# Seven half-block products in place of eight in the feed-forward stages of the second block

## The reference

```python
def _sqrelu_mlp(x, w1, w2):
    return jnp.square(jax.nn.relu(x @ w1)) @ w2
...
for l in range(DEPTH_2):          # two layers
    ...
    x = _layer_norm(ALPHA * x + h, ln_g[l, 0], ln_b[l, 0], LN_EPS)
    x = _layer_norm(ALPHA * x + _sqrelu_mlp(x, mlp_w1[l], mlp_w2[l]), ln_g[l, 1], ln_b[l, 1], LN_EPS)
```

## Time and profile before

| | |
|---|---|
| median of 3 runs | 3240.03 us |
| all runs | 3239.92, 3240.03, 3252.42 us |
| the profiled execution, its own time | 3255.05 us |
| its span, first to last instruction | 3253.3 us |
| PE busy, share of the span | 2929.4 us, 90% |
| DVE busy, share | 815.3 us, 25% |
| ACT busy, share | 530.7 us, 16% |
| DMA, mean over the span | 60 GB/s |
| granted TensorE clock, mean | 0.924 of 2.4 GHz |

### The profile page before, as it was taken

The page is one execution under the profiler, slowest core; times in us unless marked ns, Lnnn a source line. Parts: engine busy times, 40 slices in busy tenths (PEclk is TensorE's granted clock), DMA queues, the critical chain, the costliest instruction groups (busy, mean ns, idle before and its releaser), DMA issues. The chain is left out here.

```text
span 3253.3 us, 39654 instructions
## 1 busy us (share of the span) xinstructions
PE 2929.4 (90%) x17796; PEld 1594.8 (49%) x17796; DVE 815.3 (25%) x1355; ACT 530.7 (16%) x1003; POOL 216.3 (7%) x176
## 2 busy tenths in 40 slices
PE   3999988977899998897888789999989998899997
PEld 2655677753444443344766534444434454344443
DVE  1121233452444401203666420100010162110001
ACT  2111212220100001012444210000010161100001
POOL 0000044520000000001222100000000000000000
PEclk7899868998899999998888789999989999899998
DMA  5122200011122112111000011222212201122110
GB/s 250 52 104 104 78 2 2 2 79 49 55 78 78 54 71 96 64 65 52 3 3 3 2 52 52 78 78 78 78 53 104 78 1 52 52 78 78 61 69 26
DMA packets 16184, 195.91 MB, mean 60 GB/s; under 512 B 1768, under 2 KB 1896, under 8 KB 4112
## 3 DMA queue, kind: packets, MB, share of 16 engines
q1 hardware_dynamic: 16016, 193.39, 15.9%
HBM read 191.27 MB, written 2.12 MB: 59 GB/s over the span
## 5 line engine op out<-in xcount | busy, mean ns | idle before, releaser
L224 PE MATMUL psum<-arena,weight_ring 128*128 128x512 f32 x4128 | 1796.9, 598 | 78.9 <-PEq L1476 28.6
L224 PEld LDWEIGHTS psum<-arena,weight_ring 128*128 128x128 f32 x4128 | 791.3, 192 | 1079.7 <-issue 1063.2
L411 PE MATMUL psum<-arena,weight_ring 128*128 128x512 f32 (+1 forms) x672 | 244.8, 526 | 0.0
L411 PEld LDWEIGHTS psum<-arena,weight_ring 128*128 128x128 f32 x672 | 128.1, 191 | 113.5 <-issue 107.9
L1502 ACT ACTIVATE arena<-arena 128x512 f32<-128x512 f32 x48 | 29.4, 628 | 829.4 <-DVE arena L1526 584.8
L2381 DVE SCALAR_TENSOR_TENSOR arena<-arena,psum 128x512 f32<-128x512 f32 x32 | 22.0, 688 | 542.1 <-PE psum L224 542.1
L1608 DVE SCALAR_TENSOR_TENSOR arena<-psum,vecs_sb,arena 128x441 f32<-128x441 f32 (+2 forms) x176 | 122.3, 695 | 99.3 <-ACT arena L1590 93.9
L2425 DVE TENSOR_TENSOR arena<-arena 128x512 f32<-128x512 f32 x64 | 44.3, 693 | 407.2 <-ACT arena L2419 407.2
L1826 POOL TENSOR_TENSOR arena<-arena,consts_sb 128x512 f32<-128x512 f32 x48 | 64.5, 1350 | 1058.1 <-ACT arena L2118 825.6
L2419 ACT ACTIVATE arena<-psum 128x512 f32<-128x512 f32 x64 | 38.2, 597 | 408.6 <-PE psum L224 408.6
L481 DVE SCALAR_TENSOR_TENSOR arena<-psum,vecs_sb,arena 128x511 f32<-128x511 f32 x68 | 40.9, 636 | 179.6 <-ACT arena L447 178.9
(11 more groups left out here) (335 smaller groups left out, 2519.8 us busy)
## 6 DMA issues: line engine op xcount, KB each, us to landing
weight_ring<-in_mlp_up SPq DMA_DIRECT2D x16, 2048.0 KB, 7.9
weight_ring<-in_mlp_down SPq DMA_DIRECT2D x16, 2048.0 KB, 7.9
weight_ring<-in_ada SPq DMA_DIRECT2D x12, 2048.0 KB, 9.7
weight_ring<-in_gate_up SPq DMA_DIRECT2D x11, 2048.0 KB, 7.9
weight_ring<-in_w_in SPq DMA_DIRECT2D x7, 2048.0 KB, 11.4
weight_ring<-in_down SPq DMA_DIRECT2D x8, 1408.0 KB, 5.8
weight_ring<-in_w_o SPq DMA_DIRECT2D x4, 2048.0 KB, 8.0
weight_ring<-in_w_kv SPq DMA_DIRECT2D x4, 2048.0 KB, 8.4
```

Of the source, the lines that this page charges most:

```text
L224: mm = pe.matmul(bank[:, 0:width], w[:, k, m * P:(m + 1) * P], rhs(k), start=(k == 0), stop=(k == kt - 1))
L411: mm = pe.matmul(g.banks[2 * (group % 3) + off][:, 0:width], w[:, k, m * P:(m + 1) * P], h[:, k, lo:lo + width], start=(k == 0), stop=(k = ...
```

## The change

Each of the two products is cut into 2 x 2 blocks (weights by halves of the input and the output features, activations by halves of the features and of the 512 tokens) and computed by Winograd's form of Strassen's scheme: seven products of half blocks, 256 columns wide, where the plain way has eight. The sums of weight blocks are made by DVE: one into an arena buffer `s1`, three in place in the ring slot. The sums of activation blocks are made by DVE too: four at the stage's start (`up_t`), and for the down part in `hidden(c)` as the hidden tiles come (`t1`, `t2`) and, once, between the parts (`up_t` again). Product i of a chunk goes into PSUM bank i, so seven banks are in use. ACT only copies bank 0; DVE combines the banks (`up_first`, `up_others`, `down_first`, `down_others`), and does the ReLU and the square in one instruction (`hidden`, L2562). The up part and the down part stand in one block, over 16 chunks. A down output group takes two chunks, accumulated in the banks. The host lays the weights out by quarters (`quartered`); bytes and number of chunks stay as they were.

```diff
 def mlp(g):
-    x, hid, relu = view(g, X_AT, KD, SEQ), view(g, 0, KF2, SEQ), view(g, NORM_AT, 2, SEQ)
...
+    UP, ALL = 8, 16
+
+    def quads(c):
+        k = 4 if c < UP else 8
+        w = g.slots[(chunk0 + c) % RING][:, 0:SLOT].rearrange("p (k h n) -> p k h n", k=2 * k, h=2)
+        s1 = view(g, MLP_S1_AT, k, 1024 // k)
+        return w[:, 0:k, 0, :], w[:, k:2 * k, 0, :], w[:, 0:k, 1, :], w[:, k:2 * k, 1, :], s1
...
-                stream_weights(g, sp, 8)
+                stream_weights(g, sp, ALL)
 
             @block.tensor
             def _(pe):
-                group = group0
-                for i in range(8):
-                    group = gemm(g, pe, chunk0 + i, group, KD, 512, [(0, lambda k: x[:, k, :], SEQ)])
+                def product(c, i, left, right):
+                    up, r = c < UP, c if c < UP else UP + (c - UP) // 2
+                    first, last = up or c % 2 == 0, up or c % 2 == 1
+                    if first and r >= 1:
+                        if i == 0:
+                            pe.wait_ge(s.p1, r)
+                        elif i == 6:
+                            pe.wait_ge(g.acc_free, free_groups(r))
+                        else:
+                            pe.wait_ge(s.took, 6 * (r - 1) + (0, 1, 3, 5, 2, 6)[i])
+                    for pair in ((0, 1) if up else (0,)):
+                        k = 4 if up else 8
+                        for j in range(k):
+                            mm = pe.matmul(g.banks[i][:, pair * HALF:(pair + 1) * HALF], left[:, j, pair * P:(pair + 1) * P],
+                                           right(j), start=first and j == 0, stop=last and j == k - 1)
+                    if i < 6:
+                        mm.then_inc(s.prod, 1)
+                    else:
+                        mm.then_inc(g.acc_ready, 4 if up else 1)
+
+                for c in range(ALL):
+                    a11, a12, a21, a22, s1 = quads(c)
+                    landed(pe, c)
+                    if c < UP:
+                        b11, b21, b22 = (lambda j: x[:, j, lo]), (lambda j: x[:, 4 + j, lo]), (lambda j: x[:, 4 + j, hi])
+                        r1, r2, r3, r4 = (lambda j, t=t: t[:, j, :] for t in up_t)
+                    else:
+                        j0 = 8 * (c % 2)
+                        pe.wait_ge(s.hid, 5 * (4 * (c % 2) + 4))
+                        b11, b21 = (lambda j: hid[:, j0 + j, lo]), (lambda j: hid[:, 16 + j0 + j, lo])
+                        b22, r3 = (lambda j: hid[:, 16 + j0 + j, hi]), (lambda j: hid[:, j0 + j, hi])
+                        r1, r2, r4 = (lambda j: t1[:, j0 + j, :]), (lambda j: t2[:, j0 + j, :]), (lambda j: t4_of(j0 + j))
+                    product(c, 0, a11, b11)
+                    product(c, 1, a12, b21)
+                    pe.wait_ge(s.sums, 4 * c + 1)
+                    if c == 0:
+                        pe.wait_ge(s.side, 1)
+                    product(c, 2, s1, r1)
+                    pe.wait_ge(s.sums, 4 * c + 2)
+                    if c == 0:
+                        pe.wait_ge(s.side, 2)
+                    product(c, 3, a21, r3)
+                    pe.wait_ge(s.sums, 4 * c + 3)
+                    if c == 0:
+                        pe.wait_ge(s.side, 3)
+                    product(c, 4, a11, r2)
+                    if c == 0:
+                        pe.wait_ge(s.side, 4)
+                    if c >= UP:
+                        pe.wait_ge(s.side4, 2 + 2 * (c % 2))
+                    product(c, 5, a22, r4)
+                    pe.wait_ge(s.sums, 4 * c + 4)
+                    product(c, 6, a12, b22)
 
             @block.scalar
             def _(act):
-                for i in range(KF2):
-                    act.wait_ge(g.acc_ready, group0 + i + 1)
-                    if i >= 2:
-                        act.wait_ge(s.squared, i - 1)
-                    act.activation(relu[:, i % 2, :], g.banks[2 * ((group0 + i) % 3)][:, :], ACT.Relu).then_inc(g.acc_free, 1)
+                def first_product(c, r, width):
+                    act.wait_ge(s.prod, 6 * c + 1)
+                    if r >= 1:
+                        act.wait_ge(s.took, 6 * (r - 1) + 2)
+                    if r > UP:
+                        act.wait_ge(s.added, 4 * (r - UP - 1) + 1)
+                    act.activation(p1.rearrange("p a n -> p (a n)")[:, 0:width], g.banks[0][:, 0:width],
+                                   ACT.Copy).then_inc(s.p1, 1)
+
+                for c in range(UP):
+                    first_product(c, c, SEQ)
+                for m in range(4):
+                    first_product(UP + 2 * m + 1, UP + m, HALF)
             @block.vector
             def _(dve):
-                for i in range(KF2):
-                    dve.wait_ge(g.acc_free, group0 + i + 1)
-                    dve.tensor_tensor(hid[:, i, :], relu[:, i % 2, :], relu[:, i % 2, :], ALU.mult).then_inc(s.squared, 1)
-                dve.wait_ge(s.squared, KF2)
-    g.used += 8
-    g.groups += KF2
-    residual_product(g, 8, KF2, P, hid)
+                def weight_sums(c):
+                    a11, a12, a21, a22, s1 = quads(c)
+                    landed(dve, c)
+                    if c >= 1:
+                        dve.wait_ge(s.prod, 6 * (c - 1) + 3)
+                    dve.tensor_tensor(s1, a21, a22, ALU.add).then_inc(s.sums, 1)
+                    dve.wait_ge(s.sums, 4 * c + 1)
+                    dve.tensor_tensor(a21, a11, a21, ALU.subtract).then_inc(s.sums, 1)
+
+                def second_sum(c):
+                    a11, a12, a21, a22, s1 = quads(c)
+                    dve.wait_ge(s.sums, 4 * c + 2)
+                    dve.wait_ge(s.prod, 6 * c + 1)
+                    dve.tensor_tensor(a11, s1, a11, ALU.subtract).then_inc(s.sums, 1)
+
+                def fourth_sum(c):
+                    a11, a12, a21, a22, s1 = quads(c)
+                    dve.wait_ge(s.sums, 4 * c + 3)
+                    dve.wait_ge(s.prod, 6 * c + 2)
+                    dve.tensor_tensor(a12, a12, a11, ALU.subtract).then_inc(s.sums, 1)
+
+                def half_bank(i):
+                    return g.banks[i][:, :].rearrange("p (a n) -> p a n", a=2)
+
+                def rows_of(c, q):
+                    return hid[:, 16 * q + 2 * c:16 * q + 2 * c + 2, :]
+
+                def up_first(c):
+                    dve.wait_ge(s.p1, c + 1)
+                    dve.wait_ge(s.prod, 6 * c + 2)
+                    dve.tensor_tensor(rows_of(c, 0)[:, :, lo], half_bank(1), p1, ALU.add).then_inc(s.took, 1)
+
+                def up_others(c):
+                    dve.wait_ge(s.prod, 6 * c + 5)
+                    dve.tensor_tensor(u2, half_bank(4), p1, ALU.add).then_inc(s.took, 1)
+                    dve.wait_ge(s.took, 6 * c + 2)
+                    dve.tensor_tensor(v, half_bank(2), u2, ALU.add).then_inc(s.took, 1)
+                    dve.wait_ge(s.took, 6 * c + 3)
+                    dve.tensor_tensor(rows_of(c, 1)[:, :, hi], half_bank(3), v, ALU.add).then_inc(s.took, 1)
+                    dve.tensor_tensor(u2, half_bank(3), u2, ALU.add).then_inc(s.took, 1)
+                    dve.wait_ge(s.took, 6 * c + 5)
+                    dve.wait_ge(s.prod, 6 * c + 6)
+                    dve.tensor_tensor(rows_of(c, 1)[:, :, lo], half_bank(5), u2, ALU.add).then_inc(s.took, 1)
+                    dve.wait_ge(g.acc_ready, group0 + 4 * c + 4)
+                    dve.tensor_tensor(rows_of(c, 0)[:, :, hi], half_bank(6), v, ALU.add).then_inc(g.acc_free, 4)
+
+                def hidden(c):
+                    dve.wait_ge(s.took, 6 * c + 6)
+                    dve.wait_ge(g.acc_free, group0 + 4 * c + 4)
+                    for q in (0, 1):
+                        h = rows_of(c, q)
+                        dve.scalar_tensor_tensor(h, h, 0.0, h, ALU.max, ALU.mult).then_inc(s.hid, 1)
+                    dve.wait_ge(s.hid, 5 * c + 2)
+                    at = slice(2 * c, 2 * c + 2)
+                    h11, h12, h22 = rows_of(c, 0)[:, :, lo], rows_of(c, 0)[:, :, hi], rows_of(c, 1)[:, :, hi]
+                    dve.tensor_tensor(t1[:, at, :], h12, h11, ALU.subtract).then_inc(s.hid, 1)
+                    dve.wait_ge(s.hid, 5 * c + 3)
+                    dve.tensor_tensor(h12, h22, h12, ALU.subtract).then_inc(s.hid, 1)
+                    dve.tensor_tensor(t2[:, at, :], h22, t1[:, at, :], ALU.subtract).then_inc(s.hid, 1)
...
+                x11, x12, x21, x22 = x[:, 0:4, lo], x[:, 0:4, hi], x[:, 4:8, lo], x[:, 4:8, hi]
+                weight_sums(0)
+                dve.tensor_tensor(up_t[0], x12, x11, ALU.subtract).then_inc(s.side, 1)
+                dve.tensor_tensor(up_t[2], x22, x12, ALU.subtract).then_inc(s.side, 1)
+                dve.wait_ge(s.side, 2)
+                dve.tensor_tensor(up_t[1], x22, up_t[0], ALU.subtract).then_inc(s.side, 1)
+                for c in range(ALL):
+                    second_sum(c)
+                    if c == 0:
+                        dve.wait_ge(s.side, 3)
```

(78 more changed lines are left out.)

7 lines of the change are left out of this document (6 added, 1 removed).

## The result

The changed kernel took 3131.67 us (median of 4 runs, 3123.52 to 3141.42) against 3240.18 us before (median of 4; the prediction had three of them, 3240.03): a ratio of 0.9657, 95% interval 0.9622 to 0.9693. The forecast was 3129 us, within 3118 to 3155.

The account below looks back on a forecast made before the run. PE's matmul cadence was taken as the limit, all else hidden behind it. 890.1 us against 777.8 gains 112.3, less 0.6 for the tail is 111.7, taken as 111: from the median 3240.03 to 3129 us, range 3118 to 3155.

Parts of the forecast that it names:

- The matmuls: In each feed-forward stage, 1792 records of 256 columns replace 1024 of 512, at 0.2157 us each: 386.7 us a stage.
- The low clock at the start: Low clock at the feed-forward stages' starts adds 2.9 us in the first stage and 1.5 in the second.
- The border: Between a stage's up and down parts, PE's idle 2.05 and 2.04 us goes, with the low clock following it once.
- DVE: In the feed-forward stages DVE's added work stays hidden behind PE; busy time near 1130 us, smallest slack 6.9 us.
- the row with up to 2.91: The only profile row for a sum of two ring operands without PSUM, 1.18 to 2.91 us; the prediction took 1.22.
- The tail: After each stage's last matmul, 0.49 + 0.42 us and a wait replace one 0.69 us eviction: 0.3 us more, twice.
- Losses at product borders: Rival: waits at 224 product borders in the feed-forward stages each stop PE, losing 45 us: 3174 us; chance 0.07.
- DVE late: Rival: DVE's sums in the feed-forward stages end too late for PE; at 27.8 us a chunk no gain; chance 0.02.
- The weight load sets the pace: Rival: in the narrow matmul stream the load, hidden by only 0.024 us a record, raises the cadence; chance 0.03.
- without a visible gap: In `stage_in_proj`, 17 weight loads of narrow matmuls take 3.64 us, read as 0.192 us each with no gap.
- Load and stream one behind the other: Weight load and stream in series in the feed-forward stages: 0.402 us a record, 3796 us; chance 0.01.
- The price per 0.01 us: Each 0.01 us of higher cadence in the feed-forward matmuls would cost 36 us; at 0.2469 us the gain is gone.

Follow-up runs that it names:

- Experiments 2: The kernel before, all eight products, with each 512-column matmul in the feed-forward stages split into two of 256 columns: 3241.83 us, ratio 0.9994.
- 4: The changed kernel with seven products in the up part alone and the plain down part of before in its own block: 3199.03 us, ratio 0.9868.
- experiment 5: The kernel before with the up and down parts in one block and all eight products: 3234.53 us, ratio 0.9977.
- experiments 6: The changed kernel with six more DVE additions of 512 elements ahead of `second_sum`, chunks 1 to 8 of each stage: 3127.48 us, ratio 0.9652.
- 7: The changed kernel with twelve more DVE additions of 512 elements ahead of `second_sum`, chunks 1 to 8 of each stage: 3161.04 us, ratio 0.9765.
- experiment 3: The changed kernel with the up part's matmuls narrowed from 256 to 128 columns, each with its weight load: 3145.8 us, ratio 0.9696.
- warming matmuls: The changed kernel with six matmuls on constants ending PE's norm lists: all norms 3130.32 and 3136.56 us, the two ahead of feed-forward stages alone 3125.89 us.

## Why the prediction was right

**The matmuls**, the term that carries all: forecast 1792 x 0.2157 + 0.17 = 386.7 us a stage; measured 0.21584, so 387.0. The cadence of 16 narrow records between wide ones held for 1792 in a row. Experiments 2, 4 and 5 leave the missing eighth of the products as the cause of the gain: the narrower matmuls by themselves give none, the border gives 4 to 6 us, and the up part alone gives its own share.

**The low clock at the start**: forecast 2.9 and 1.5 us; measured 3.0 and 2.9 (389.99 and 389.85 us from first to last matmul, less 387.0). The 1.5 was carried over from the second stage of the profile before, which had lost less at its start (221.45 against 222.9 us); another execution need not repeat that. The prediction's sum was 111.7 us before it was rounded, and the profile has 109.7: 1.4 us of the difference are this, 0.1 the first stage's start and 0.5 the cadence.

**The border**: gone in both stages, 4 to 6 us (experiment 5). It could go because the first down chunk needs only the hidden tiles of the first four up chunks.

**DVE**: hidden, as costed. In the timeline of the changed kernel `hidden` of chunk 0 and then `second_sum` of chunk 1 (which starts at 1965.09 - 6.90 = 1958.19) end at 1964.81, 6.6 us after the chunk's start, forecast 6.9:

```profile
1958.46 0.69 DVE L2555 TENSOR_TENSOR arena<-psum,arena 128x512 f32<-128x512 f32 x1 [2.76 <-PE psum L2452]
1959.25 2.36 DVE L2562 SCALAR_TENSOR_TENSOR arena<-arena 128x1024 f32<-128x1024 f32 x2
...
1963.59 1.22 DVE L2524 TENSOR_TENSOR weight_ring<-arena,weight_ring 128x1024 f32<-128x1024 f32 x1
```

Its busy time is 1113.4 us, forecast near 1130: a scalar_tensor_tensor of 1024 elements takes 1.22 us where 1.29 was taken, and two instructions without a wait between them overlap a little (2.36 us for the two of `hidden`, forecast 2.58). The sum of two blocks in the ring took 1.22 us, so the row with up to 2.91 was no measure for it; POOL's work on the ring there is my guess for the cause, which was not tested.

**The tail**: 0.3 us longer, as forecast (1.54 and 1.53 us ahead of L1453, before 1.24, shown above, and 1.26).

**The rivals.** Losses at product borders: no idle time at any of them. DVE late: slack measured (experiments 6 and 7). The weight load sets the pace: right that it doesn't, wrong in the reason. The prediction gave the load 0.024 us of margin, taking its shown 0.192 us as its pace, and called it thin; experiment 3 shows at least 0.104 us of margin (0.2158 - 0.1117) at the same load duration. The reading that 17 loads ran "without a visible gap" was of a merged row: 17 loads in 3.64 us begin 0.2157 us apart, with 0.02 us between the end of one and the start of the next. Load and stream one behind the other, 0.402 us a record, is ruled out by the measured 0.2158. The price per 0.01 us is arithmetic, and no run tested it.

**What was luck.** The median came out 3 us from the forecast, closer than the forecast could promise: the four runs of the changed kernel spread over 18 us, and its two repetitions have medians of 3129.22 and 3127.96 us. The profiled executions differ by another 22 us in code that didn't change.

## What to carry to other kernels

Where PE is bound by its own stream in one unbroken row, fewer columns are worth what they are at the cadence, and the cadence of another width can be read from any short run of that width in the trace; here 16 records foretold 1792 to 0.1%. A weight load's duration in the trace is no pace: compare the distance of the starts. Before paying for sums on another engine, write down for each of its results when it is ready and when it is wanted within one period; the smallest difference (7 us a chunk here) is what can still be added.

## What the runs showed of the hardware

Records, each with a full 128 x 128 weight load, follow each other after 0.4293, 0.2159 and 0.1117 us at 512, 256 and 128 columns, and the trace shows the load with the same 0.19 us at all three widths (0.192, 0.190 and 0.192). At 128 columns the loads overlap each other by their shown times.

An unchanged stage differs from one execution to the next by more than most terms here. In `stage_rwkv_mix`, first and last start of the same 16 matmuls (kernel before, then the changed kernel in its first, second and third profile):

```profile
L1864 PE MATMUL psum<-arena x16: 589/626/693, 1506.8 to 1770.1; 64*128 64x512 f32 x16
```

```profile
L1864 PE MATMUL psum<-arena x16: 589/626/693, 1501.1 to 1750.8; 64*128 64x512 f32 x16
```

```profile
L1864 PE MATMUL psum<-arena x16: 589/626/693, 1504.2 to 1753.9; 64*128 64x512 f32 x16
```

```profile
L1864 PE MATMUL psum<-arena x16: 589/626/693, 1505.5 to 1768.7; 64*128 64x512 f32 x16
```

That is 263.3, 249.7, 249.7 and 263.2 us, so it doesn't hang on the change: the changed kernel shows both. The windows over the first two show the difference in the clock column, at like work of DVE, ACT and POOL:

```profile
1506.80:1770.10 263.30, 203.62 (x4734) 169.70 (x4734) 157.31 (x263) 106.50 (x166) 62.87 (x46) 0.82 0.03 10
```

```profile
1501.10:1750.80 249.70, 189.91 (x4732) 159.37 (x4734) 158.57 (x262) 106.36 (x166) 62.90 (x46) 0.87 0.03 11
```

In this stage PE works in short pieces, and how much of it runs at the low level varies. It makes up 13.5 of the 17.9 us between the changed kernel's first and third profiled executions (3123.52 and 3141.44 us). In the three profiles with warming matmuls the stage took 262.5, 266.8 and 262.5 us, the middle one without any such matmul ahead of it. Of the ten profiles without them, five have 249.7 us and the other five 256.5 to 263.3, so a long stage comes without warming too, and three long ones in a row may well be chance; that stays open. Whoever measures a gain under 10 us in this kernel with four or five runs should read it from the stage's own rows.
